# Row scaling of products, staged gelu and a three-part scan step in the second block of a two-block transformer

## The reference, cut to what matters

```
h  = concat(meta, x)                                   # 272 x 2048
z  = rmsnorm(h, mix_norm) @ w_in                       # u | q_a | kv_a | k_pe
ya = s5_mixer(u)        # complex scan over 272 positions, y = Re(C h) + d*u,
                        # g = gelu(y); ya = g * sigmoid(g @ w_glu + b)
yb = mla_mixer(q_a, kv_a, k_pe)                        # 8 heads, scores masked by chunk
y  = concat(rmsnorm(ya, out_norm_ssm), rmsnorm(yb, out_norm_attn))
h  = h + y @ w_out
t  = rmsnorm(h, ffn_norm) @ w_up                       # gate | val, 2 x 5504
h  = h + (silu(conv3(t_gate) + b) * t_val) @ w_down
out = rmsnorm(h, final_norm)[16:]
```

## Time and profile before

| | |
|---|---|
| median of 3 runs | 3252.51 us |
| the profiled execution, its own time | 3260.05 us |
| its span | 3258.1 us |
| PE busy | 2969.1 us (91%) |
| DVE busy | 1911.4 us (59%) |
| ACT busy | 1131.7 us (35%) |
| POOL busy | 390.2 us (12%) |
| mean granted clock of TensorE | 0.937 of full |

### The profile page before, as it was taken

The page is one execution under the profiler, slowest core; times in us unless marked ns, Lnnn a source line. Parts: engine busy times, 40 slices in busy tenths (PEclk is TensorE's granted clock), DMA queues, the critical chain, the costliest instruction groups (busy, mean ns, idle before and its releaser), DMA issues.

```text
span 3258.1 us, 40376 instructions
## 1 busy us (share of the span) xinstructions
PE 2969.1 (91%) x15557; PEld 2397.9 (74%) x15557; DVE 1911.4 (59%) x3332; ACT 1131.7 (35%) x1810; POOL 390.2 (12%) x397
## 2 busy tenths in 40 slices
PE   7978998989889978989997978978989999999998
PEld 2447677877667866768776767754688999999887
DVE  3228778676767665452453547777455666666444
ACT  3232322323223234232342443222334444444443
POOL 5760000000100000000001003545000000000000
PEclk9989999999889999999999988886598999999999
DMA  8846245353434653232332443321043555555665
GB/s 323 275 145 209 81 143 190 107 169 100 136 126 159 223 201 117 90 105 91 117 115 85 149 139 109 121 89 51 15 142 120 185 186 183 181 182 183 200 193 168
DMA packets 151393, 480.60 MB, mean 148 GB/s; under 512 B 17040, under 2 KB 18064, under 8 KB 150032
## 3 DMA queue, kind: packets, MB, share of 16 engines
q1 hardware_dynamic: 138816, 435.22, 40.7%
q10 hardware_dynamic: 9824, 33.88, 2.8%
q0 software_dynamic: 2560, 8.91, 0.9%
HBM read 464.84 MB, written 13.11 MB: 147 GB/s over the span
## 4 chain that ended last, share of the span: by engine, by line
PE 49%; DVE 8%; issue 3%; ACT 3%; DMA 2%; POOL 1%; DVEq 0%; ACTq 0%; SPq 0%; POOLq 0%
PE bank L1012 14%; PE bank L1014 14%; PE bank L1013 14%; DMA first_block_work<-w_mod_cols 1%; ACT split_weights L2013 1%; DVE split_weights L1334 1%; PE bank L1205 1%; PE bank L1268 1%; PE bank L1220 1%; PE bank L1212 1%; PE bank L1127 0%; PE bank L1247 0%; PE bank L1248 0%; PE bank L1213 0%; DVE common L1454 0%
## 5 line engine op out<-in xcount | busy, mean ns | idle before, releaser
L1334 DVE TENSOR_TENSOR split_weights<-common,split_weights 128x1024 fp32r<-128x1024 f32 x636 | 791.8, 1253 | 711.4 <-ACT split_weights L2013 683.9
L2013 ACT ACTIVATE split_weights<-common 128x1024 fp32r<-128x1024 f32 x636 | 664.3, 1053 | 929.9 <-PE bank L1014 877.0
L1012 PE MATMUL bank<-split_weights,features 128*128 128x512 f32 x1920 | 808.0, 421 | 50.3 <-DVE first_block_work L1541 15.6
L1014 PE MATMUL bank<-split_weights,features 128*128 128x512 f32 x1920 | 762.4, 397 | 0.0
L1013 PE MATMUL bank<-split_weights,features 128*128 128x512 f32 x1920 | 761.6, 397 | 0.0
L1012 PEld LDWEIGHTS bank<-split_weights,features 128*128 128x128 f32 x1920 | 369.1, 192 | 167.6 <-issue 54.6
L1013 PEld LDWEIGHTS bank<-split_weights,features 128*128 128x128 f32 x1920 | 369.3, 192 | 79.5 <-issue 11.3
L1014 PEld LDWEIGHTS bank<-split_weights,features 128*128 128x128 f32 x1920 | 367.8, 192 | 81.1
L1012 PE MATMUL bank<-ffn_input_split,split_weights 128*128 128x256 f32 (+1 forms) x1376 | 391.6, 285 | 3.3 <-DVE ffn_input_split L1778 1.6
L1013 PE MATMUL bank<-ffn_input_split,split_weights 128*128 128x256 f32 (+1 forms) x1376 | 390.4, 284 | 0.0
L1014 PE MATMUL bank<-ffn_input_split,split_weights 128*128 128x256 f32 (+1 forms) x1376 | 390.0, 283 | 0.0
(11 more groups left out here) (294 smaller groups left out, 3428.0 us busy)
## 6 DMA issues: line engine op xcount, KB each, us to landing
common<-w_in SPq DMA_DIRECT2D x260, 512.0 KB, 3.3
common<-w_up SPq DMA_DIRECT2D x172, 512.0 KB, 4.2
first_block_work<-w_mod_cols SPq DMA_DIRECT2D x256, 256.0 KB, 3.7
common<-w_out SPq DMA_DIRECT2D x96, 512.0 KB, 3.3
common<-w_down SPq DMA_DIRECT2D x84, 512.0 KB, 4.1
old_stream<-w_mod SPq DMA_DIRECT2D x64, 512.0 KB, 5.0
trig<-common ACTq DMA_DIRECT2D x32, 272.0 KB, 4.6
second_block_work<-trig POOLq DMA_DIRECT2D x32, 272.0 KB, 3.6
```

The lines of the kernel that those rows point to most:

```text
L1012: e.matmul(out_ap, xs[0], ws[0], start=first, stop=False)
L1014: return e.matmul(out_ap, xs[0], ws[1], start=False, stop=last)
L1334: e.tensor_tensor(lo, raw, hi.bitcast(F32), ALU.subtract).then_inc(*low_done.tick(("lo", m)))
L2013: e.activation(split_slots[:, 0, i, 0:words], raw_slots[:, m % RAW, 0:words], ACT.Copy).then_inc(*high_done.tick(("high", m)))
```

## The change

1. **Row scaling of products.** For mix, attn, ssm and ffn the split inputs are now features times gain only: `gain_high` (ACT: copy with the gain as scale) and `gain_low` (DVE: features times gain minus the high part, one operation). The row goes through `row_mean`, `row_turn` and `row_spread` while products run, is kept in SBUF by ACT (`kept_rows`), and multiplies the products: in `in2_out` (now DVE), in `add_h` (now two DVE operations) and in `gated` (two more DVE operations; ACT's first term reads the scaled copy). qa and kva keep the old way (`norm_features`), their rows spread one tile later.
2. **Order.** Finishing steps of products are held until the row is kept; square sums of the glu, ssm and ffn parts come two to four tiles late, those of the last ffn features in the first up tile (`later`). `h_turn` is followed by the gain of the same feature; b_blocks, the squares' mean and c_blocks stand between the first input products. The ssm features go to the second half of `x_s`, and the ssm row's epsilon is 16 times as large, since `glu` now leaves its factor of one half out (twice with gelu's).
3. **Gelu in stages.** Three stages, each one DVE operation and one of ACT's at most, put between advances, and the splitting of g (`split_g` before) as stages 3 and 4.
4. **Scan.** A step is three advances: scan_in to scan_load with a shaping stage; the next feed with a shaping stage; scan_read. `side(work)` has a weight, 2.9 for a piece of columns, 1.5, 0.8 and 1.4 for q, k and v, 2.0 for a unit of the scores; the pace stays 0.5 to the end of the attn output products, so that the scan runs beside these too.
5. **Meta load** is issued in layer 1, after the stream's reload, and not after new_h.
6. Buffers in the work area are laid out anew; `gelu_t`, `rows2`, `g_gate`, `g_val`, `row3`, `half_row` are new.

```diff
-    def side(self):
+    def side(self, work=1.0):
         self.clock += 1
+        while self.delayed and self.delayed[0][0] <= self.clock:
+            self.do(*self.delayed.pop(0)[1])
...
-            self.credit += self.pace
-            if self.credit >= 1.0:
+            self.credit += self.pace * work
+            while self.side_work and self.credit >= 1.0:
...
+    def gained(self, name, f):
+        self.do("gain_high", name, f)
+        self.gained_end()
+        self.to_gain.append(("gain_low", name, f))
...
         for f in range(KT):
             self.do("h_turn", f, 3 + f % 5, self.copies())
+            self.gained("mix", f)
...
+            if i == 0:
+                self.do("h_mean")
+                self.do("b_blocks")
+            if i == 1:
+                self.row_turn("mix")
+                self.do("row_spread", "mix")
+                self.do("c_blocks")
...
+            if ct >= spread_at:
+                while held and (held[0][2] < ct or ct == KT - 1):
+                    self.added(*held.pop(0))
+            if name == "ssm" and ct > 3:
+                self.sum_squares("ffn", ct - 4, KT, 7)
...
+    def added(self, *step):
+        self.do(*step)
+        if step[1] == "ssm":
+            self.gained("ffn", step[2])
...
         def add_h(name, ct, bank):
-            e.tensor_tensor(h_t[:, ct, Q0:T2], h_t[:, ct, Q0:T2], banks[bank][:, 0:TQ], ALU.add).then_inc(
-                *block_made.tick((after, ct), ("free", "columns", "out2", name, ct)))
+            e.tensor_tensor(t, banks[bank][:, 0:TQ], kept_rows[name][:, 0:TQ], ALU.mult).then_inc(
+                *block_made.tick(("free", "columns", "out2", name, ct)))
+            e.wait_ge(*block_made.last())
+            e.tensor_tensor(h_t[:, ct, Q0:T2], h_t[:, ct, Q0:T2], t, ALU.add).then_inc(*block_made.tick((after, ct)))
...
         def gated(f, bg, bv):
+            for s, n in seen.new(at("columns", "up_g", f), at("conv", f - 2) if f > 1 else START):
+                e.wait_ge(s, n)
+            e.tensor_tensor(gate, banks[bg][:, 0:TQ], row3, ALU.mult).then_inc(
+                *gates_made.tick(("gate_scaled", f), ("free", "columns", "up_g", f)))
+            for s, n in seen.new(at("columns", "up_v", f)):
+                e.wait_ge(s, n)
+            e.tensor_tensor(val, banks[bv][:, 0:LAT], half_row[:, META - Q0:TQ], ALU.mult).then_inc(
+                *gates_made.tick(("free", "columns", "up_v", f)))
```

More of the change, by code:

```diff
@@ L626, in scan @@
                 if (step - 1) % 4 == 3:
-                    i = (step - 1) // 4
-                    self.do("gelu", i, tuple(self.rb))
-                    self.rb[1] = ("g_ready", i)
+                    shaping.extend(((step - 1) // 4, stage) for stage in range(3))
+            yield
+        while shaping or splitting:
+            shape()
+            yield
     def columns(self, use, bank, pieces, x, x0, t0, t1):
@@ L724, in second_block @@
             self.do("glu", ct, bank)
[L725 to L736, removed]
+            self.gained("ssm", ct)
@@ L744, in feed_forward @@
-    def feed_forward(self):
-        self.do("ffn_begin")
-        self.squares, self.norm_tmp, self.rb = {}, {}, [None, None]
-        self.norm("ffn", KT, 7, summed=True)
+            self.columns(("out2", name, ct), bank, 1, name, ST, 0, TQ)
+            held.append(("add_h", name, ct, bank))
+            if summed < ST:
+                for f in range(summed, min(summed + 4, ST)):
+                    self.sum_squares(name, f, ST, sums)
+                summed = min(summed + 4, ST)
+                if summed == ST:
+                    self.row_mean(name, ST, sums)
+                    self.row_turn(name)
+                    spread_at = ct + 1
+            elif ct == spread_at:
+                self.do("row_spread", name)
@@ new lines, in gain_low @@
+        def gain_low(name, f):
+            src, _, _, gain, dst, d_f, t0, t1, ready = norms[name]
+            for s, n in seen.new(at("gain_high", name, f), at(ready, f)):
+                e.wait_ge(s, n)
+            hi = dst[:, 0, d_f + f, 0:t1 - t0].bitcast(F32)
+            e.scalar_tensor_tensor(out=dst[:, 1, d_f + f, 0:t1 - t0], in0=src[:, f, t0:t1], scalar=col(gain, f), in1=hi,
+                                   op0=ALU.mult, op1=ALU.subtract).then_inc(*norms_made.tick(("normed", name, f)))
@@ L1861, in mla_scores @@
                 e.wait_ge(s, n)
-            if x in (2, 3):
-                for s, n in seen.new(at("normed", "kva", x - 2)):
+            if x < 4:
+                for s, n in seen.new(at("normed", "kva", KL // P - 1), at("normed", "qa", QL // P - 1)):
                     e.wait_ge(s, n)
```

432 lines of the change are left out of this document (258 added, 174 removed).

## The result

The changed kernel took 3234.0 us by the median of five runs (3228.4 to 3240.5), the kernel before 3252.5 beside it (3250.4 to 3259.8): ratio 0.9935, 95% interval 0.9917 to 0.9953. It is faster, by 0.65% and not by the 2.6% of the forecast: 3169 us was predicted, with a range to 3210, and 3234 lies outside it.

What follows compares the result with a forecast made beforehand. The prediction saw different limits by stretch: PE waiting in the opening and for the scan, PE at half clock in the scores, mostly PE elsewhere. Its terms sum to -83.9 us off the 3252.5 median: 3169 us, range 3140 to 3210.

Steps and rivals of the forecast that it cites:

- the opening's smaller part: Opening: with the meta load in layer 1, turning the stream can start when new_h ends; 3.0 us go.
- The price of a step in the scores: Scores: a scan step costs 4.3 us at the half clock, with 9 steps instead of 5.5.
- the over 95% I named: Attention output: sign that the forecast holds, DVE busy for over 95% of the stretch.
- the DVE rival: Input products and attention output: DVE loses the waits back, saving 48 us instead of 84, 3205 us; chance 0.12.
- the clock rival: Clock raised in the scores, 3129 us, chance 0.04; or low through attention output and glu, 3211 us, chance 0.04.
- Square sums two tiles late take the 0.9 us waits: Glu and ssm norm: late square sums remove PE's waits, 40.8 us becoming 27, -13.8.
- The pieces are two ahead (some 4 us), so of 8.6 us about 5 show: Ssm output: a 3.83 us ring over PE's 3.2 a tile shows only partly; 56 us, -1.6.
- +0.05 a tile: Feed forward, 43 tiles: ring of load, high, low and chain 11.5 us against 11.46, +2 us in all.
- My upper bound, 0.5 a tile: Feed forward: upper bound of 0.5 us a tile, +21 us, if the two handings over cost 0.2 each.
- my first rival (0.11): Feed forward: the load ring bounds it; mild form 1.0 us more a tile, 43 in all, 3210 us; chance 0.11.
- The first tile, -12.5: Feed forward's norm and first tile: 21.5 us falls to 9, 5.7 for matmuls and 3.3 for PE's waits.
- the 8 that I had left to the range: Attention output: add_h's new second half, with two SBUF inputs beside POOL, would cost 16 x 0.5 = 8 us more.

Runs made afterwards that it cites:

- e6: The kernel before with only the meta load's issue moved into layer 1, behind the last layer's stream reload; one execution, 3258.8 us.
- e8: e7 with the scan at a pace of 0.65 instead of 0.5 in all stretches; 3199.3 us, ratio 0.9810 to the kernel before.
- e1: Changed kernel with, in the glu, the square of tile ct-2 first on ScalarE, ahead of the tanh and gained high part; 3211.5 us.
- e5: Changed kernel with, in the ssm output, the row's product and sum of tile ct-1 ahead of the low part on VectorE; 3220.4 us.
- e2: Changed kernel with, in the ssm output, the square of tile ct-4 on ScalarE ahead of tile ct-1's gained high part; 3220.4 us.
- e4: Changed kernel with the feed forward's gating as before the change, leaving out the multiplication by the norm's row (output differs, timing only); 3202.8 us.
- e7: Changed kernel with four order changes together, those of e1, e2, e3 and e5; 3173.6 us, ratio 0.9737 to the kernel before.
- e3: Changed kernel with the feed forward's gating in two parts, the second issued after the next tile's first piece of products; 3209.6 us.

## Why the prediction was wrong

Five of its terms held, and they are the part of the change it was made of: opening -26.7 (forecast -26.4), input products -14.1 (-11.5), q, k, v -47.1 (-49.9), scores +11.3 (+15.4), attention output +13.5 (+14.4), together -63.1 against -58.0. e6 confirms the opening's smaller part, and e8 that the attention output falls to PE's 56 us once the scan is over. The price of a step in the scores is not confirmed: some 3.5 steps more came for 11.3 us, 3.2 each and not 4.3, and e8's came dearer for POOL's sake. In the attention output the terms of VectorE's step add up to 10.3 us and not to the 10.7 of the forecast, so that with the right sum it is 75 us against 77.1 measured. The clock in the scores stayed at 0.57, as forecast. VectorE in the attention output is busy for 90%, not the over 95% I named, though the length came out within a microsecond; that sign was too strict, with handing over on both sides of each operation. The products did move up, and neither the DVE rival nor the clock rival took place as written: the attention output ran at 0.95, and the glu's 0.85 went with its waits in e1.

Four terms failed, by 63 us together, and three of them on one kind of error:

- **"Square sums two tiles late take the 0.9 us waits"** (glu, -13.8; measured +5.0). I looked at how old the square's input is, not at what stands ahead of it on ScalarE. Deferring an instruction in an in-order queue puts it behind younger work: its own input was ready two tiles before, and it left when the tanh of the newest products had been through. e1 shows it: same instruction, other place, 26.7 us. The low clock after most of these waits, which I hadn't counted at all, made it nearly twice as dear. The Trainium skill, page "TensorE: Matmul & The Clock Gate", section "HAM oscillation — how this bites in real kernels", describes tiles that each begin at the low clock because each is preceded by a wait. The trace agrees in part: tiles behind a wait ran at 0.64, but they began at the high clock and fell within their first products, and the waits here (1.88 us) are shorter than the page's of some 3 to 5 us. I had used that page for the scores, and not here.
- **"The pieces are two ahead (some 4 us), so of 8.6 us about 5 show"** (ssm output, -1.6; measured +10.3). The ring was found and its 3.83 us were nearly right (3.92). But a ring of two other engines that is longer than PE's tile shows in full in each tile once the lead is used up, and the lead was used up at once, by the start-up wait (4.25 us), when four held sums and their squares came in one go. e5 and e2 show both.
- **Feed forward, "+0.05 a tile"** (+2; measured +30.6 to the end of the span). The row's product, ScalarE's step and their handing over added 1.10 us to VectorE's way to the next low part (from 3.87 in the earlier trace rows to 4.97), where I had 0.81. The slack was 0.81: behind a late load e4 has tiles of 10.65 us, the ring's own period then, against PE's 11.46. (By the forecast's own rows it is 0.92, 2751.92 against 2746.62 + 1.18 + 3.2, where it says 0.8.) So 0.29 are left and show in every tile: 11.75 us is about the least that occurs, 42 x 0.29 = 12 us. My upper bound, 0.5 a tile, was bracketing that. What it left out is the other 15 us of the 42 tiles, most of it in nine of 12.6 to 13.6, and 3 us at the span's two ends. In seven of the nine the load that the ring waits for lands in 4.1 to 5.1 us, not in 3.0 to 3.4 as in the rest; the other two come right behind such a tile, follow waits of PE of 1.84 and 1.86 us and have a granted clock of 0.87. Loads that land late are nothing new; the landing times are those of the earlier trace rows's line over the whole feed forward, before and after:

```profile
DMA to landing us min/median/max: 3.1/4.2/6.2
```

```profile
DMA to landing us min/median/max: 3.0/4.4/6.3
```

  Before, a late load cost a tile of 12.2 or 12.9 us, and the next took 10.7: the slack made it up. Without slack it stays: 13.4, then 11.7 (or, with the low clock, 13.6, then 13.2). That is the mild form of my first rival (0.11), 0.66 us a tile instead of its 1.0, though by another way: the loads take hardly longer than before (4.4 by the median instead of 4.2), only nothing makes the late ones up.
- **The first tile, -12.5** (measured -8.8): one more 1.83 us wait for a square, which e2's and e5's orders take away together, down to 16.4 us in e7. What is left over the forecast's 14.7 was not tested; 2.4 us of the stretch, from 2460.5 to 2462.9, are the spreading of the norm's row between the fourth piece and the fifth.

The four orders of e7 take 58 us off these stretches (60 off the median, 3234 to 3174), and with them the forecast's 3169 is nearly there. So what was wrong was not what the change removes, but that I took three places, in which it puts work into a queue, as free.

## What to carry to other kernels

Where a change adds or defers an instruction, write down the order of that engine's queue and ask what the instruction ahead of it waits for; the age of its own input says nothing. Close the rings (high part, low part, sum, high part; or load, split, gating, load) and compare the period with the engine that sets the tile: well below it a ring costs nothing (10.65 us under 11.46, in e4), a little below it late loads cost something (11.07 in e3 and e7: 5 to 6 us over the 42 tiles), and above it every tile pays in full and each late load is kept for good. The cure is often order alone: e7 does the same work as the changed kernel and takes 60 us less.

## What the runs showed of the hardware

- Waits of 1.88 us of PE, one in each 7 us tile, were followed by half clock in most of the next tile: 24 products took 4.7 us instead of 3.2. It was not so every time: of the five times 24 products behind such a wait the first (from 2350.1 us) ran at full clock, and that tile took 5.5 us. In the ssm output, with waits of 0.33 us in each 3.9, the products kept 3.2.
- PE busy for 101.5 of 110.9 us of scores stays at 0.57 (transposes are 13.7 us of it), and so it does in e7 and e8, with the scan's parts at either pace. What raises it there was not tested.
- A DVE operation with two SBUF inputs paid little for POOL beside it. The new sum (line 2012) and the row's product (2009, one input in PSUM) in the attention output, with POOL busy for 37.7 of 77.1 us, and in the ssm output, POOL nearly idle (mean ns behind the busy time):

```profile
L2012 DVE TENSOR_TENSOR common<-common,second_block_work 128x258 f32<-128x258 f32 x14 | 6.8, 483 | 0.5
L2009 DVE TENSOR_TENSOR second_block_work<-bank,second_block_work 128x258 f32<-128x258 f32 x15 | 6.2, 416 | 0.1
```

```profile
L2009 DVE TENSOR_TENSOR second_block_work<-bank,second_block_work 128x258 f32<-128x258 f32 x16 | 6.7, 422 | 2.9 <-ACT second_block_work L2403 2.6 <-PE bank L1104 0.2
L2012 DVE TENSOR_TENSOR common<-common,second_block_work 128x258 f32<-128x258 f32 x15 | 6.4, 428 | 0.5
```

  The sum takes 0.055 us more, 0.9 us for 16, not the 8 that I had left to the range; the product takes no more. In kind that is the rule of the Trainium skill, page "SBUF — State Buffer", section "Who interferes with whom"; for the size the low part's extra (4 times as long an operation) was a poor measure.
